# Adding a token's two fetched expert rows: two diagonal products on TensorE, or a weighted sum ahead of one product

## The reference

```
g_sel = argmax(g_logits); e_in = e_logits[g_sel]; top_v, top_i = top_k(e_in, 2)
top_w = softmax(top_v) * g_w                        # two weights per token
y = sum over the two experts: gate * (silu(h @ w_gate[e]) * (h @ w_up[e])) @ w_down[e]
x = layer_norm(ALPHA * x + gate2 * y) * ln2_w + ln2_b
```

## Time and profile before

| | us |
|---|---|
| median of 3 timed runs (lowest, highest) | 1128.86 (1126.47, 1131.48) |
| the profiled execution, its own time | 1126.7 |
| its span in the profile | 1124.9 |
| TensorE busy | 1049.8 (93%) |
| VectorE, ScalarE, GpSimd busy | 424.9, 215.3, 178.0 |
| mean granted share of TensorE's clock | 0.98 |

### The profile page before, as it was taken

One profiled execution on the slowest core, in us unless ns is written; L12 is line 12 of the kernel. 1 busy time (PEld: TensorE's weight loads), 2 busy tenths in 40 slices (PEclk: granted clock), 3 DMA queues, 4 the chain that ended last, 5 costly groups with the idle time before them and its releaser, 6 DMA issues.

```text
span 1124.9 us, 16702 instructions
## 1 busy us (share of the span) xinstructions
PE 1049.8 (93%) x6678; PEld 698.0 (62%) x6679; DVE 424.9 (38%) x1033; ACT 215.3 (19%) x536; POOL 178.0 (16%) x183
## 2 busy tenths in 40 slices
PE   5999999999999999989899999999999989899995
PEld 1865777658856555556548567785687645555642
DVE  0034645346763121221154345442578512121215
ACT  0322324301011111111112323341001101111111
POOL 0133302023101111111111200200501111111111
PEclk8899999999999999999999999999999999999998
DMA  8955942389799999999989822226897899999993
GB/s 356 270 142 119 380 184 90 138 287 351 295 420 419 418 419 418 418 418 417 421 311 265 288 75 76 89 77 235 291 425 288 338 419 418 419 419 420 416 392 148
DMA packets 102625, 342.78 MB, mean 305 GB/s; under 512 B 20300, under 2 KB 61308, under 8 KB 70420
## 3 DMA queue, kind: packets, MB, share of 16 engines
q1 hardware_dynamic: 88400, 313.47, 72.2%
q0 software_dynamic: 12416, 18.79, 5.6%
q10 hardware_dynamic: 1732, 9.45, 2.1%
HBM read 337.76 MB, written 28.25 MB: 325 GB/s over the span
## 4 chain that ended last, share of the span: by engine, by line
PE 71%; DMA 16%; DVE 6%; ACT 2%; issue 2%; POOL 1%; SPq 1%; POOLq 0%; ACTq 0%; DVEq 0%
PE ps L1053 17%; PE ps L1361 12%; DMA expert_rows<-arena 9%; PE ps L1046 8%; PE ps L1385 5%; PE ps L1237 3%; DMA ring<-in_exp_w_down 3%; PE ps L993 3%; DMA small<-in_exp_w_up 3%; PE ps L1229 2%; DMA x<-in_x_prompt 2%; PE ps L1327 2%; PE ps L1319 2%; PE ps L1436 2%; PE ps L1146 1%
## 5 line engine op out<-in xcount | busy, mean ns | idle before, releaser
L1361 PE MATMUL ps<-ring,arena 128*64 128x256 f32 x1248 | 198.3, 386 | 16.5 <-ACT arena L1747 15.5
L1053 PE MATMUL ps<-ring,arena 128*128 128x256 f32 (+1 forms) x960 | 198.4, 364 | 2.1 <-ACT arena L1685 2.1
L1053 PEld LDWEIGHTS ps<-ring,arena 128*128 128x128 f32 x960 | 169.2, 193 | 24.8 <-issue 5.1
L1361 PEld LDWEIGHTS ps<-ring,arena 128*64 128x64 f32 x1248 | 120.9, 139 | 64.2 <-ACT arena L1747 17.8
L1385 PE MATMUL ps<-ring,arena 128*64 128x512 f32 x344 | 108.5, 594 | 3.6 <-DMA ring<-in_exp_w_down 2.6
L1361 PE MATMUL ps<-arena 128*64 128x256 f32 x448 | 101.0, 381 | 4.8 <-ACT arena L1747 2.7
L1046 PE MATMUL ps<-arena,ring 128*128 128x384 f32 x288 | 96.9, 490 | 0.5 <-ACT arena L1690 0.5
L2275 DVE TENSOR_TENSOR arena<-arena,ps 128x256 f32<-128x256 f32 x32 | 13.5, 421 | 199.6 <-ACT arena L1752 199.6
L2559 POOL DMA_INDIRECT arena<-token_rows,arena x30 | 30.6, 1019 | 314.1 <-PE ps L1327 123.4
L1046 PEld LDWEIGHTS ps<-arena,ring 128*128 128x128 f32 x288 | 53.3, 190 | 36.6 <-issue 1.8
L1361 PEld LDWEIGHTS ps<-arena 128*64 128x64 f32 x448 | 60.2, 137 | 24.3 <-issue 3.8
(11 more groups left out here) (311 smaller groups left out, 1473.6 us busy)
## 6 DMA issues: line engine op xcount, KB each, us to landing
ring<-in_exp_w_down SPq DMA_DIRECT2D x44, 1024.0 KB, 21.2
ring<-in_w_mod SPq DMA_DIRECT2D x43, 1024.0 KB, 6.9
ring<-in_exp_w_gate SPq DMA_DIRECT2D x41, 1024.0 KB, 19.3
ring<-in_exp_w_up SPq DMA_DIRECT2D x39, 1024.0 KB, 19.4
ring<-in_w_in SPq DMA_DIRECT2D x24, 1024.0 KB, 13.3
arena<-in_exp_w_gate SPq DMA_DIRECT2D x14, 1024.0 KB, 22.4
arena<-in_exp_w_up SPq DMA_DIRECT2D x14, 1024.0 KB, 21.0
arena<-in_exp_w_down SPq DMA_DIRECT2D x12, 1024.0 KB, 22.7
```

What stands on the lines that cost most here:

```text
L1053: mm = pe.matmul(out[:, 0:w], hT[:, ch, where * P:(where + 1) * P], unit(l, name)[:, ch, 0:w], start=(ch == 0), stop=(ch == CH - 1))
L1361: mm = pe.matmul(ps[64 * w:64 * w + 64, i % 2, kind * FF:(kind + 1) * FF], xgT[i % 2][:, ch, w * SLOTS:(w + 1) * SLOTS], weights[:, ch * F ...
```

## The change

A tile's two fetched rows are weighed ahead of TensorE: ScalarE scales the second row of each token by its weight in place, VectorE multiplies the first by its weight and adds the second, and TensorE adds this sum to the last pair's part by one product with the identity. The diagonal matrices go, and the third tile's products are all in `final_sums`. VectorE does the three sums ahead of `combine`.

The late rows come as four small loads (four partitions of 256 numbers each, into the 256 free columns of the bias tile) ahead of the expert weights; TensorE spreads them by products with one-hot columns of the identity, four rows at a time, in two rounds, one ahead of each half of the last pair's `hidden`; ScalarE copies them from PSUM to the places in the ring that the broadcasts wrote. Two semaphores of the first pair become one.

```diff
+LATE_BANKS = ((PAIRS - 2) % 2, 2, 3, MARKS_BANK)
...
+        def late_source():
+            return bias[:, :, :, :].rearrange("p h r c -> p (h r c)")[:, UNIT:UNIT + 256]
...
-            def load_late(l, name):
-                wait_released(sp, *SPOT[l, ("late", name)][2])
+            def load_late(l):
+                wait_released(sp, l, ("arena", BIAS_PLACE))
                 for k in range(2):
-                    if name == "ln2":
-                        sp.dma_start(late_tile(l, "ln2", k), (ln2_w, ln2_b)[k][l:l + 1].to_broadcast([P, D]))\
-                            .then_inc(ln2_in.sem, 16)
-                    else:
-                        sp.dma_start(late_tile(l, "gate2", k), modd[l, 1, k:k + 1, D:2 * D].to_broadcast([P, D]))\
-                            .then_inc(gate2_in.sem, 16)
+                    sp.dma_start(late_source()[32 * k:32 * k + 4, :],
+                                 modd[l, 1, k, D:2 * D].rearrange("(q n) -> q n", q=4)).then_inc(bias_in.sem, 16)
+                for k, row in enumerate((ln2_w, ln2_b)):
+                    sp.dma_start(late_source()[32 * (2 + k):32 * (2 + k) + 4, :],
+                                 row[l, :].rearrange("(q n) -> q n", q=4)).then_inc(bias_in.sem, 16)
...
                 load_rows(l, "ctx2")
                 load_rows(l, "lat2")
+                load_late(l)
                 for unit in early_units(l + 1) + EXPERT_LOADS:
...
+            def late_rows(l, n):
+                if n == 0:
+                    pe.wait_ge(bias_in.sem, bias_in.at(l, bias_in.step))
+                    pe.wait_ge(pt_copied.sem, pt_copied.at(l, 1))
+                    pe.wait_ge(hid_ready.sem, hid_ready.at(l, PAIRS - 1))
+                    pe.wait_ge(xt_act.sem, xt_act.at(l, PAIRS))
+                    pe.wait_ge(xt_dve.sem, xt_dve.at(l, PAIRS))
+                else:
+                    pe.wait_ge(late_copied.sem, late_copied.at(l, 1))
+                for q in range(2):
+                    for g in range(4):
+                        rows4 = slice(32 * g, 32 * g + 4)
+                        col = K_ID + 32 * g + 2 * n + q
+                        mm = pe.matmul(ps[:, LATE_BANKS[g], 256 * q:256 * q + 256], kc[rows4, col:col + 1].to_broadcast([4, P]),
+                                       late_source()[rows4, :], start=True, stop=True)
+                mm.then_inc(late_ready.sem, 1)
...
             def final_sums(l):
-                pe.wait_ge(pt_copied.sem, pt_copied.at(l, 1))
-                pe.wait_ge(diag_ready.sem, diag_ready.at(l, 1))
+                pe.wait_ge(late_copied.sem, late_copied.at(l, 2))
                 pe.wait_ge(row_act.sem, row_act.at(l, PAIRS))
                 pe.wait_ge(row_dve.sem, row_dve.at(l, PAIRS))
                 last_rows(l, 0)
                 last_rows(l, 1)
-                pe.wait_ge(gathered[0].sem, gathered[0].at(l, 16))
                 for n in range(2):
-                    for k in range(2):
-                        mm = choice(l, 0, k, n)
-                    mm.then_inc(final_ready.sem, 1)
-                pe.wait_ge(gathered[1].sem, gathered[1].at(l, 16))
-                final_choice(l, 1, 0)
-                final_choice(l, 1, 1)
+                    other_rows(l, 0, n).then_inc(final_ready.sem, 1)
                 last_rows(l, 2)
-                pe.wait_ge(gathered[2].sem, gathered[2].at(l, 16))
-                final_choice(l, 2, 0)
+                for t in (1, 2):
+                    other_rows(l, t, 0)
+                    other_rows(l, t, 1).then_inc(final_ready.sem, 1)
...
+            def other_rows(l, t, n):
+                if n == 0:
+                    pe.wait_ge(summed.sem, summed.at(l, t + 1))
+                return pe.matmul(ps[:, FINAL_BANKS[t][n], :], ident, gath(l, t)[:, 0, 512 * n:512 * n + 512],
+                                 start=False, stop=True)
...
+                    if i == PAIRS - 1:
+                        late_rows(l, 0)
                     hidden(l, i, 0)
+                    if i == PAIRS - 1:
+                        late_rows(l, 1)
...
-                    if l and kind == "job" and i == JOB_NO["pN", 0, 0]:
-                        final_choice(l - 1, TILES - 1, 1)
...
+            def copy_late_rows(l, n):
+                act.wait_ge(late_ready.sem, late_ready.at(l, n + 1))
+                if n == 0:
+                    for name in ("gate2", "ln2"):
+                        wait_released(act, *SPOT[l, ("late", name)][2])
+                for g in range(4):
+                    ins = act.activation(late_tile(l, ("gate2", "ln2")[g // 2], g % 2)[:, 512 * n:512 * n + 512],
+                                         ps[:, LATE_BANKS[g], :], ACT.Copy)
+                ins.then_inc(late_copied.sem, 1)
...
                     if i == PAIRS - 2:
                         rows_half(l, i)
+                        copy_late_rows(l, 0)
+                        copy_late_rows(l, 1)
...
                 rows_half(l, PAIRS - 1)
+                act.wait_ge(weights_masked.sem, weights_masked.at(l, 1))
+                for t in range(TILES):
+                    second = gath(l, t)[:, 1, :]
+                    act.wait_ge(gathered[t].sem, gathered[t].at(l, 16))
+                    act.activation(second, second, ACT.Copy, scale=wtsm[:, 1, t:t + 1]).then_inc(scaled.sem, 1)
...
+            def weigh_rows(l, t):
+                one, second = gath(l, t)[:, 0, :], gath(l, t)[:, 1, :]
+                dve.wait_ge(gathered[t].sem, gathered[t].at(l, 16))
+                dve.wait_ge(scaled.sem, scaled.at(l, t + 1))
+                dve.scalar_tensor_tensor(one, one, wtsm[:, 0, t:t + 1], second, ALU.mult, ALU.add).then_inc(summed.sem, 1)
...
-                for t in range(TILES):
-                    for k in range(2):
-                        ins = dve.tensor_scalar(diag(k, t), ident, wtsm[:, k, t:t + 1], None, ALU.mult)
-                ins.then_inc(diag_ready.sem, 1)
                 rows_half(l, PAIRS - 1)
-                dve.wait_ge(gate2_in.sem, gate2_in.at(l, gate2_in.step))
+                for t in range(TILES):
+                    weigh_rows(l, t)
+                dve.wait_ge(late_copied.sem, late_copied.at(l, 2))
                 if l + 1 < DEPTH:
                     for t in range(TILES):
                         combine(l, t, chain)
                         normalise(l, t, chain)
```

More of the change, by code:

```diff
@@ L567, in item_rows @@
             return item_place_of(l, ITEM_UNITS)[:, k * D:(k + 1) * D]
-        def diag(k, t):
-            return xgT[1][:, 2 * t + k, :]
         def gath(l, t):
@@ L621, in build @@
         N_SMALL = 16
-        small_in, bias_in = signal("small_in", 16 * N_SMALL), signal("bias_in", 32)
-        rows_in, ln2_in = signal("rows_in", 16 * 8), signal("ln2_in", 32)
-        gate2_in = signal("gate2_in", 32)
+        small_in, bias_in = signal("small_in", 16 * N_SMALL), signal("bias_in", 32 + 64)
+        rows_in = signal("rows_in", 16 * 8)
+        late_ready, late_copied = signal("late_ready", 2), signal("late_copied", 2)
         diff_out, results_out = signal("diff_out", 32), signal("results_out", 16 * 4)
@@ L678, in build @@
         first_ready = signal("first_ready", 2)
-        first_act, first_dve = signal("first_act", 1), signal("first_dve", 1)
+        first_copied = signal("first_copied", 2)
         xt_ready = signal("xt_ready", 2 * PAIRS)
@@ L701, in build @@
         rows_zeroed = signal("rows_zeroed")
-        diag_ready, final_ready = signal("diag_ready", 1), signal("final_ready", TILES + 1)
+        scaled, summed, final_ready = signal("scaled", TILES), signal("summed", TILES), signal("final_ready", TILES + 1)
         var2, rstd2, ln2_done = signal("var2", TILES), signal("rstd2", TILES), signal("ln2_done", TILES)
@@ L878, in bias_loads @@
                     wait_released(sp, *LAST_IN[l - 1][BIAS_PLACE])
+                    sp.wait_ge(late_copied.sem, late_copied.at(l - 1, 2))
                 one = bass.ds(l, 1)
@@ L962, in _ @@
                                 load_item(l, o0, i)
-                    elif unit[0] == "late":
-                        load_late(l, unit[1])
-                    elif unit[0] != "item" and unit[0] != "gath":
+                    elif unit[0] not in ("item", "gath", "late"):
                         load(l, unit)
@@ L1330, in first_rows_T @@
             def first_rows_T(l):
-                pe.wait_ge(first_act.sem, first_act.at(l, 1))
-                pe.wait_ge(first_dve.sem, first_dve.at(l, 1))
+                pe.wait_ge(first_copied.sem, first_copied.at(l, 2))
                 for b in range(2):
@@ L1613, in _ @@
                 final_sums(l)
-            final_choice(DEPTH - 1, TILES - 1, 1)
         def drain_to(kind, what, where):
@@ L1841, in _ @@
                 act.wait_ge(first_ready.sem, first_ready.at(l, 1))
-                act.activation(xr[0][:, 0:512], ps[:, ROWS_BANK, :], ACT.Copy).then_inc(first_act.sem, 1)
```

(17 more changed lines are left out.)

## The result

The changed kernel takes 1132.78 us (median of 20 runs, 1127.47 to 1136.59), the kernel before 1129.22 (20 runs, 1125.71 to 1131.77): a ratio of 1.0034, 95% interval 1.0022 to 1.0045. It is slower by some 3.6 us, 2.5 to 5.1. That is the size of rival (a), and one of its two reasons held: the gathers did land sooner, but the clock did fall.

A forecast was written before the change was run, and what follows sets the result against it. TensorE, busy 93% of the span, and the chains of waits at the layer ends were taken to bound the kernel. 2.7 + 1.0 + 4.2 = 7.9 us on 1126.7 gave 1134.6, with half of 2.2 added 1135.7; range 1127 to 1142.

The forecast's parts named there:

- rival (a): Both layers' ends: same loss but small; clock does not fall, gathers land 1 us earlier; +4.9, 1132.7; chance 0.28.
- The order in layer 0: End of layer 0: tile 0's norm stands behind the third gather, so layer 1's projection starts 2.7 us later.
- A third gather that lands over 2 us sooner after its issue: Layer ends: a sign named as showing the forecast wrong; before, layer 0's third gather landed 11.6 us after issue.
- (b): Both layers' ends: the broadcasts' 2.1 MB all go to the third gather; -1.5 us, 1126.3; chance 0.10.
- The clock: Behind TensorE's 6.1 us hole at layer 0's end: granted clock falls, +1.0 us, bounds 0 and 1.7.
- The spread: Last pair of each layer: 1.0 us per spread; 0 in layer 0, +2.0 in layer 1, bounds 1.7 and 7.2.
- rival (c): Spreads in both layers: row groups do not overlap, 3.46 us each; +17.0, 1144.8; chance 0.06.
- Layer 1's end: VectorE at layer 1's end: work that started at 1108.64 starts at 1112.85, +4.2 us, the spread's 2.0 within it.
- The late rows: SP's queue, both layers: broadcasts of 2.1 MB a layer leave; this can only bring the gathers forward.
- (d): Layer 0's last weights come earlier without broadcasts, by up to 2.1 us; 1134.6; chance 0.56 together with the forecast.
- The base: Whole kernel: profiled execution 1126.7 us, plus half of the 2.2 by which the median of three timed runs exceeds it.
- The case called likeliest: Whole kernel: slower by more than about 0.5% (5.6 us); chance 0.62.

The follow-up runs named there:

- e3: The changed kernel plus ten idle TensorE products of 256 columns in the hole ahead of layer 1's first transposes: 1129.13 us, ratio 0.9998.
- e4: The changed kernel with VectorE's sum of tile 2 moved behind its first work on tile 0: 1127.65 us, ratio 0.999 to the kernel before.
- e6: The kernel before with late rows spread by TensorE in layer 0 alone, broadcasts in layer 1, diagonal products kept: 1126.49 us, ratio 0.9974.
- e1: The kernel before with the small loads and spread in both layers, diagonal products kept: 1129.04 us, ratio 1.0002.
- e11: e6 once more, unchanged, for a second profile and more times: 1125.87 us, ratio 0.9983.
- e10: The kernel before with late rows spread by TensorE in layer 1 alone, broadcasts in layer 0, diagonal products kept: 1132.40 us, ratio 1.0026.
- e2: The kernel before with the weighing by ScalarE and VectorE alone; late rows still broadcast in both layers: 1137.89 us, ratio 1.0089.

## Why the prediction was right, and in its size not

- **The order in layer 0** (+2.7 forecast): right in kind, 1.4 measured (e3 less before; e4 undoes it). The mis-sized term is the third fetch: 11.8 us from the first issue to the landing was taken from layer 1, and it was 9.74 (566.41 + 8.88 - 565.55). Layer 1 of before, said to have "little beside them", was no measure of fetches alone: 0.34 MB of the broadcasts still moved beside their first 4.2 us. That 2.1 us alone would leave 0.6 of the 2.7; the way from VectorE's start on tile 0 to the projection was 0.5 longer than forecast (from 578.54 to 588.81 in e3, 10.27 us against 9.75), and some 0.3 stay open. Of VectorE's work on tile 0 the 7.75 us were right: from 577.76 to 585.53. A third gather that lands over 2 us sooner after its issue was named as a sign of being wrong, and in layer 0 it came (8.9 us against 11.6): the reason of (b) was right in part, and the order outweighed it.
- **The clock** (+1.0, bounds 0 and 1.7): 2.6 (9.51 - 6.91), 2.5 by e3, outside the bounds. Their prices came from a pair's products in layer 1, and I assumed that part of the slow stretch would fall into waiting. Here it fell on the projection, which lies on the path in full length. The sum of the two steps, 3.7 forecast and 3.9 measured, was right only by luck: the errors cancelled.
- **The spread**: 1.07 to 1.08 us each against 1.0, so the four row groups run side by side and rival (c) fell. In layer 0 it costs nothing where TensorE waits for the last pair's weights: from the last but one pair's `down` to `last_rows` e6 takes 20.41 us and before 20.51. In the profiles of after and e1 that wait is not there and the spread stands on the chain, the case for which the prediction had 2.0. In layer 1 it costs 2.44 instead of 2.0. The two rows hold 2.15 of that; the other 0.3 lie in the rows beside them (3.60 and 3.63 in e1, 6.93 for both in the earlier trace rows), at the four changes of shape, under 0.1 us for one. This agrees with the rule weighed there, that a change of tiling mode drains TensorE (the Trainium skill, TensorEngine Tiling (Array Packing), Key Properties), as far as a cost can show it.
- **Layer 1's end** (+4.2, the spread within it, so 2.2 beyond): 0.71 beyond. The third fetch landed 10.3 us after the first issue (1101.57 + 8.1 - 1099.38), 1.5 less than I took; that is the difference.
- **The late rows** (only the gathers gain): this is the gain that was missed. "Their leaving can only bring the gathers forward" left out that they could matter to a part of the kernel that comes later. It is worth some 2.5 us in a median run (e6, e11, e10), and no rival had it: (b) put the gain on the gathers and (d) on layer 0's last weights.
- **The base.** I went by one execution (1126.7) and added half its distance to the median. Both kernels' medians are now known from 20 runs, 1129.2 and 1132.8.

Added up: 3.9 + 2.4 + 0.7 at the ends, less some 2.5 in the loop, is 4.5 us, and the times say 3.6 (2.5 to 5.1). The case called likeliest, slower by over 0.5%, did not come: it is slower by 0.34%, clear of no change, but inside that bound. The mechanism of the loss, VectorE's order, the clock behind it and the spread in layer 1, was the right one. Three sizes were off, the third fetch above all, and one gain was missed; that the time lies within the range owes something to luck, as the sizes cancelled in part.

## What to carry to other kernels

When a sum moves to an engine whose program has it ahead of all its other work, look where its last operand arrives: put the work on the last tile behind the first work on the first, or every tile waits for the last transfer. Price a hole in TensorE by what runs right behind it: if that lies on the path, the lower clock costs something of its own, here 2.5 us behind a hole of 4.87. And judge a transfer that is taken away by times of the whole kernel too, one layer at a time: what it gave here does not show at its own place.

## What the runs showed of the hardware

- A TensorE hole of 4.87 us was followed by 7 us at a granted clock of 0.51, while it stayed at 1.00 where twenty instructions (4.48 us) filled most of that hole (e3). At nearly the same start of the projection (588.15 and 588.81) its 32 instructions took 9.51 and 7.14 us.
- The clock also fell without a hole: from 339 to 345 in after it was 0.72, though TensorE had been busy throughout; its last work before that were 44 instructions of 4 columns (336.38 to 339.71). In before the same instructions were followed by 1.00.
- Products of four rows each in four row groups run side by side: sixteen instructions of 256 columns took 1.07 us, where one full product's instruction of that size takes 0.216 (6.91/32), so sixteen in a row 3.46.
- Three fetches of 1 MB ended 9.74 and 10.3 us after the first issue without broadcasts ahead of them (after), and 11.8 to 13.2 with them (before and e2). These 1.5 to 3.5 us are less than the 5.0 that the broadcasts' 2.1 MB take at 0.416 MB/us, so the fetches did not wait for all of them.
- Scatters of 128 rows beside the weights of layer 1 took 9.4 to 11.3 us from issue to landing (the first five on the chain of each profile), and the second and fifth of them were at least 0.3 us shorter in every profile without layer 0's broadcasts than in any with them. Why is open.
